# Two layers of attention and a 16-expert mixture on one core: four full sets of expert weights that go round, and each expert's blocks in one loop of their own in the second layer

## The reference

```python
SEQ = 256; CTX_LEN = 256; D_MODEL = 1024; DEPTH = 2
N_EXPERTS = 16; TOP_K = 2; EXPERT_FF = 512

def moe_ffn(h, router_w, router_bias, w_gate, w_up, w_down):
    ...
    _, exp_idx = lax.top_k(jnp.where(exp_mask, sel, NEG_INF), TOP_K)
    ...
    y = jnp.zeros_like(h)
    for e in range(N_EXPERTS):
        a = jax.nn.silu(h @ w_gate[e]) * (h @ w_up[e])
        y = y + gates[:, e:e + 1] * (a @ w_down[e])
    return y
```

## Time and profile before

| | us |
|---|---|
| median of 3 runs | 1149.88 (1148.8 to 1151.57) |
| the profiled execution, its own time | 1146.06 |
| its span, first to last instruction | 1144.2 |
| first mixture, TensorE's block work | about 418 to 649 |
| between (combination, second attention) | about 650 to 906 |
| second mixture | about 906 to 1136 |

### The profile page before, as it was taken

How to read it: one execution, slowest core, us unless ns; L and a number is a source line. 1 busy time by engine, 2 the same in 40 slices (tenths; PEclk the granted TensorE clock), 3 DMA queues, 4 the chain that set the end, 5 groups by cost and what they waited for, 6 DMA issues and landing times.

```text
span 1144.2 us, 25209 instructions
## 1 busy us (share of the span) xinstructions
PE 1004.0 (88%) x10134; PEld 660.9 (58%) x10135; DVE 411.6 (36%) x881; ACT 336.5 (29%) x755; POOL 173.1 (15%) x257
## 2 busy tenths in 40 slices
PE   4799999988889988799899649999999866999875
PEld 2577777544555565467566447888454643555543
DVE  1533331355843542122122273212862721323212
ACT  3532221366741211011111255323861110111111
POOL 0000000000000024244344300920000010112100
PEclk9999999999999999899899869999999897999988
DMA  9866664998240579999999467222627889699994
GB/s 338 303 219 221 221 210 171 346 355 314 109 199 18 208 280 399 422 421 424 422 424 415 172 248 164 94 74 104 264 60 306 335 320 425 253 381 425 424 423 188
DMA packets 90811, 317.58 MB, mean 278 GB/s; under 512 B 20094, under 2 KB 32135, under 8 KB 78451
## 3 DMA queue, kind: packets, MB, share of 16 engines
q1 hardware_dynamic: 84594, 303.04, 69.0%
q0 software_dynamic: 5280, 10.36, 2.4%
q10 hardware_dynamic: 864, 3.15, 0.7%
HBM read 311.05 MB, written 9.54 MB: 280 GB/s over the span
## 4 chain that ended last, share of the span: by engine, by line
PE 73%; DMA 14%; DVE 4%; issue 4%; ACT 3%; SPq 1%; DVEq 0%; ACTq 0%; POOLq 0%
PE ps L2031 25%; PE ps L1772 21%; PE ps L1927 7%; DMA expert_sets<-in_moe_w_up_dram 7%; PE ps L1669 5%; PE ps L1693 3%; DMA expert_sets<-in_moe_w_down_dram 2%; DMA ring<-in_ada_w_dram 2%; PE ps L2053 2%; PE ps L1827 1%; PE ps L1854 1%; DMA ada_late<-in_ada_w_dram 1%; PE ps L1883 1%; PE ps L1710 1%; DMA moe<-h_rows,slot_idx 1%
## 5 line engine op out<-in xcount | busy, mean ns | idle before, releaser
L2031 PE MATMUL ps<-expert_sets,moe 128*32 128x256 f32 x6304 | 363.7, 390 | 54.1 <-issue 31.2
L2031 PEld LDWEIGHTS ps<-expert_sets,moe 128*32 128x32 f32 x6304 | 226.5, 113 | 186.7 <-issue 76.5
L1772 PE MATMUL ps<-w_high,x_high 128*128 128x512 f32 x352 | 141.4, 402 | 6.6 <-DVE x_low L508 5.1
L1618 DVE STREAM_TRANSPOSE moe<-moe 128x256 f32<-128x256 f32 x68 | 44.7, 657 | 263.8 <-PE ps L2031 257.2
L1772 PE MATMUL ps<-w_high,x_low 128*128 128x512 f32 x352 | 137.9, 392 | 0.0
L1772 PE MATMUL ps<-w_low,x_high 128*128 128x512 f32 x352 | 137.7, 391 | 0.0
L1125 ACT ACTIVATE moe<-ps 128x128 f32<-128x128 f32 x68 | 18.9, 277 | 327.5 <-PE ps L2031 325.9
L495 DVE TENSOR_TENSOR w_low<-ring,w_high 128x2048 fp32r<-128x2048 f32 x24 | 56.2, 2350 | 132.5 <-ACT w_high L492 132.5
L1772 PEld LDWEIGHTS ps<-w_high,x_high 128*128 128x128 f32 x352 | 66.5, 189 | 30.5 <-issue 14.8
L779 POOL MEMSET moe<- 128x128 f32 x2 | 0.4, 204 | 534.9 <-PE ps L1953 534.9
L797 POOL DMA_INDIRECT moe<-h_rows,gather_idx x66 | 68.4, 1037 | 52.2 <-POOL gather_idx L843 27.7
(11 more groups left out here) (261 smaller groups left out, 1143.1 us busy)
## 6 DMA issues: line engine op xcount, KB each, us to landing
expert_sets<-in_moe_w_down_dram SPq DMA_DIRECT2D x32, 2048.0 KB, 18.4
expert_sets<-in_moe_w_gate_dram SPq DMA_DIRECT2D x30, 2048.0 KB, 15.9
expert_sets<-in_moe_w_up_dram SPq DMA_DIRECT2D x30, 2048.0 KB, 21.0
ring<-in_ada_w_dram SPq DMA_DIRECT2D x16, 2048.0 KB, 8.0
ring<-in_diff_w_qkv_dram SPq DMA_DIRECT2D x6, 2048.0 KB, 9.3
ada_late<-in_ada_w_dram SPq DMA_DIRECT2D x6, 2048.0 KB, 12.4
ring<-in_na_w_qkv_dram SPq DMA_DIRECT2D x6, 2048.0 KB, 8.9
rows<-mod_rows SPq DMA_DIRECT2D x11, 512.0 KB, 7.3
```

The lines of the kernel that those rows point to most:

```text
L1618: dve.transpose(blk_inT, blk_in[b].rearrange("p (j k) -> p k j", k=KC)).then_inc(m_xt[l], 1)
L1772: mm = pe.matmul(ps[:, n % 2], x_part[:, k, tok], w_part, start=(k == 0 and i == 0), stop=(k == KC - 1 and i == 2))
L2031: mm = pe.matmul(ps[g * SLOTS:(g + 1) * SLOTS, bank, 0:n_out], lhs_T[:, k, :], weights(k, g), start=(k == 0), stop=(k == n_chunks - 1), sk ...
```

## The change

There are now four full sets. The extra pair gets a down matrix beside it (`extra_down`, 16 KB a partition), for which room is made behind the residual rows: it also covers the rows of modulation values and the rotary tables, both of which have been used by then, and the scratch area for the descriptors of GpSimd's transfers shrinks to 1024 bytes a partition. Every position uses set (position modulo 4). Its loads wait for the position four before. The down matrix of position 3 is loaded ahead: in the first layer right after the modulation rows of the second layer have been stored, in the second layer behind the attention strips. The outer loops hold four positions and run three times in both layers.

In the second layer the order of TensorE changes: for every block, gates and ups of that block, the sums of the preceding block, the downs of that same block, in one loop per position. VectorE weighs the preceding block's result at the start of its step rather than at the end. The code of positions 13 to 15 and the special last position go. The strips of the second attention take slots 0, 1, 2 in turn, so that the first two wait for gates and ups of position 14 and the third for its downs.

The diff, cut to its core:

```diff
-EXTRA = 3
+SETS, EXTRA = 4, 3
...
+        extra_down = over("extra_down", ARENA_KB + 16, [P, FF // P, D])
...
-                    add_qkv(g, (i + 2) % 3)
+                    add_qkv(g, i % 3)
...
+        def loads(l, p, rounds=0):
+
+            return 16 * (p // SETS + 1 + rounds + l * (N_EXP // SETS))
...
-            def later_parts(l, p, which, ws, back=3):
+            def later_parts(l, p, which):
                 e = expert_at(l, p)
-                for w in ws:
+                blocks = sp.value_load(plan[0:1, bass.ds(p + 1 - SETS, 1)], min_val=1, max_val=MAX_BLOCKS)
+                for w in range(3):
                     if w != 1:
-                        blocks = sp.value_load(plan[0:1, bass.ds(p + 1 - (3 if w == 2 else back), 1)], min_val=1, max_val=MAX_BLOCKS)
                         sp.wait_ge((m_gu, m_gu, m_dn)[w][l], blocks + (w == 2))
                         sp.sem_inc(s_turn_sp, 1)
-                    expert_weights(l, w, e, which[w == 2])
+                    expert_weights(l, w, e, which)
...
-                later_parts(l, EXTRA + 1, (gate_set(EXTRA + 1), None), (0, 1), back=4)
-                later_parts(l, EXTRA, (None, EXTRA % 3), (2,))
-                later_parts(l, EXTRA + 1, (None, (EXTRA + 1) % 3), (2,))
-                for p in range(5, 7):
-                    later_parts(l, p, (gate_set(p), p % 3), (0, 1, 2), back=4)
-                with sp.Fori(0, (N_EXP - 7) // 3) as i:
-                    for p in range(7, 10):
-                        later_parts(l, 3 * i + p, (gate_set(p), p % 3), (0, 1, 2))
+                with sp.Fori(0, N_EXP // SETS - 1) as i:
+                    for s in range(SETS):
+                        later_parts(l, SETS * i + SETS + s, s)
...
+            sp.wait_ge(s_modD, 32)
+            expert_weights(0, 2, EXTRA, EXTRA)
...
+            expert_weights(1, 2, EXTRA, EXTRA)
             sp.wait_ge(s_qm[1], len(qkv_jobs[1]))
...
                     for b in range(2):
+                        if l == 1:
+                            dve.wait_ge(m_dn[1], 2 * j + b + 1)
+                            weigh_rows(2 * j + b)
                         dve.wait_ge(m_ga[l][1 - b], 16 * j + 16)
...
-                        if l == 1:
-                            weigh_rows(2 * j + b)
...
+                def blocks_summed(p, first, end, rounds=0):
+
+                    with pe.Fori(first, end) as i:
+                        gates_ups(i, p % SETS)
+                        sum_rows(i)
+                        down_loaded(p, rounds)
+                        downs(i, p % SETS)
...
+                def expert_summed(p, first, end, rounds=0, then=None):
+
+                    after = None if then is None else block_end(then)
+                    gates_loaded(p, rounds)
+                    pe.sem_inc(s_turn_pe, 1)
+                    blocks_summed(p, first, end, rounds)
                     return after
...
-                keep_busy((5, 14)[l])
+                keep_busy((5, 10)[l])
...
-    nc = bacc.Bacc("TRN2", target_bir_lowering=False, num_devices=1)
+    nc = bacc.Bacc("TRN2", target_bir_lowering=False, num_devices=1, dynamic_dma_scratch_size=1024)
```

More of the change, by code:

```diff
@@ L362, in build_trunk @@
         s_idx = [sem(f"plan_ready_{l}") for l in range(LAYERS)]
-        m_wl = [[sem(f"expert_{w}_loaded_{s}") for w in ("gate", "up", "down")] for s in range(3)]
-        s_extra = sem("extra_parts_loaded")
+        m_wl = [[sem(f"expert_{w}_loaded_{s}") for w in ("gate", "up", "down")] for s in range(SETS)]
         s_keep = sem("residual_rows_kept")
@@ L729, in _ @@
             sp.dma_start(mod_dram[1].ap(), mod_rows[:]).then_inc(s_modD, 16)
-            last_blocks, n0 = load_experts(0)
-            sp.wait_ge(m_dn[0], last_blocks + 1)
-            load_strip(1, 0)
-            load_expert_rows(0, n0)
-            blocks = sp.value_load(plan[0:1, N_EXP:N_EXP + 1], min_val=N_EXP, max_val=MAX_BLOCKS)
+            sp.wait_ge(s_modD, 32)
+            expert_weights(0, 2, EXTRA, EXTRA)
+            blocks, pairs = load_experts(0)
             sp.wait_ge(m_gu[0], blocks)
-            for j in range(1, 3):
+            for j in range(2):
                 load_strip(1, j)
+            sp.wait_ge(m_dn[0], blocks + 1)
+            load_strip(1, 2)
+            load_expert_rows(0, pairs)
             sp.wait_ge(s_cb[0], NT[0])
@@ L1709, in keep_busy @@
                 for _ in range(count):
-                    pe.matmul(ps[:, 3, 0:2 * P], ident, cst[:, 0:2 * P], start=True, stop=True)
+                    pe.matmul(ps[:, 3, 0:2 * P], ident, cst[:, P:3 * P], start=True, stop=True)
             for a in range(ADA_QKV):
@@ L2105, in expert @@
                     down_loaded(p - 1, rounds)
-                    downs(first - 1, (p - 1) % 3)
-                    sum_rows(first)
+                    downs(first - 1, (p - 1) % SETS)
                     with pe.If(first + 1 < end):
@@ L2128, in _ @@
                     weight_table()
-                keep_busy((5, 14)[l])
+                keep_busy((5, 10)[l])
                 pe.wait_ge(s_idx[l], 2)
                 ends = [block_end(0), block_end(1)]
+                if l == 1:
+                    sum_rows(0)
+                    down_loaded(0)
+                    downs(0, 0)
                 with pe.If(1 < ends[0]):
                     down_loaded(0)
-                    with pe.Fori(1, ends[0]) as i:
-                        gates_ups(i, 0)
-                        downs(i - 1, 0)
-                        sum_rows(i)
@@ L2138, in _ @@
-                for p in range(1, 4):
-                    ends.append(expert(p, ends[p - 1], ends[p], then=p + 1 if p < 3 else None))
-                with pe.Fori(0, (N_EXP - 4) // 3 - l) as three:
-                    end_0, end_1 = block_end(3 * three + 3), block_end(3 * three + 4)
-                    end_2 = expert(4, end_0, end_1, three, 3 * three + 5)
-                    end_3 = expert(5, end_1, end_2, three, 3 * three + 6)
-                    expert(6, end_2, end_3, three)
-                if l == 1:
-                    end_0, end_1 = block_end(N_EXP - 4), block_end(N_EXP - 3)
-                    end_2 = expert(N_EXP - 3, end_0, end_1, then=N_EXP - 2)
-                    end_3 = expert(N_EXP - 2, end_1, end_2, then=N_EXP - 1)
-                    last_expert(N_EXP - 1, end_2, end_3)
+                    pe.sem_inc(s_turn_pe, 1)
@@ new lines, in _ @@
+                    if l == 1:
+                        blocks_summed(0, 1, ends[0])
+                    else:
+                        with pe.Fori(1, ends[0]) as i:
+                            gates_ups(i, 0)
+                            downs(i - 1, 0)
+                turn_of = (expert, expert_summed)[l]
+                for p in range(1, SETS):
+                    ends.append(turn_of(p, ends[p - 1], ends[p], then=p + 1 if p + 1 < SETS else None))
+                with pe.Fori(0, N_EXP // SETS - 1) as i:
+                    end_0, end_1 = block_end(SETS * i + SETS - 1), block_end(SETS * i + SETS)
+                    end_2 = turn_of(SETS, end_0, end_1, i, SETS * i + SETS + 1)
+                    end_3 = turn_of(SETS + 1, end_1, end_2, i, SETS * i + SETS + 2)
+                    end_4 = turn_of(SETS + 2, end_2, end_3, i, SETS * i + SETS + 3)
+                    turn_of(SETS + 3, end_3, end_4, i)
```

77 lines of the change are left out of this document (23 added, 54 removed).

## The result

The changed kernel takes **1123.81 us**, median of 5 runs (1119.17 to 1125.81), against 1149.73 (1148.67 to 1151.57) for the kernel before in the same session: a ratio of 0.9773 (95% interval 0.9755 to 0.9792). The forecast was 1123.5. The profiled execution took 1119.17 us with a span of 1117.3, where before it was 1146.06 and 1144.2.

The account below looks back on a forecast made before the run. TensorE and DMA bound the first mixture, late-started loads the second's end. Terms -5.5 (first mixture), -19.5 (second), -1.3 (tail) sum to -26.3: 1119.8 profiled, plus 3.8 to the median gives 1123.5 us; 8-in-10 range 1114 to 1138.

Parts of the forecast that it names:

- First mixture: Layer-0 mixture: one load leaves the saturated stretch, so the last up lands 5.5 us earlier; -5.5 us, ends -7.5 and 0.
- The loads of the second mixture: Second mixture: SyncE's queue no longer stands still during position 5's six blocks; loads end at 1096 to 1106, before 1129.
- The open turn: Second mixture: each block's downs wait for VectorE's turned activation, 0.40 us a block uncovered by the sums, ends 0 and 1.5.
- Entries into the outer loop: Second mixture, TensorE: three entries at 2.3 us each, with a third register read, 1.80 each before; 6.9 us.
- First pass of code: Second layer, TensorE: stalls when code runs the first time; 5 us taken, ends 0 and 16.
- Lowered clock: Second mixture: one set of gates slowed behind a first-code stop, 7.17 us instead of 5.32; 1.8 us.
- Tail: Behind the last downs: one sum instead of two, 2.0 us for weighing and sum; -1.3 us.
- The longer loop body does not stay: Rival, 8%: layer 0's four-position loop no longer stays on the chip, two more first passes; +10.6 us, 1134.
- First pass as before: Rival, 10%: the second layer's first pass stalls as before, 16 us instead of 5; +11 us, 1134.5.
- the turn longer than its pieces: Rival, 10%: the second mixture's turn leaves 0.9 us open a block instead of 0.4; +13 us, 1136.5.
- The clock falls: Rival, 7%: TensorE's stops in every second-mixture block lower its clock; nine blocks low cost 58 us, 1181.
- Scratch area: Rival, 3%: the smaller area makes GpSimd wait, about 7 us more per layer-0 block if one transfer fits; far above 1300.

Follow-up runs that it names:

- the ends carried: Changed kernel, with TensorE carrying the outer loop's two starting block ends in registers from the preceding pass, both layers: 1120.1 us, ratio 0.9735 to the kernel before.
- the two experiments on the turn: Changed kernel, second layer: VectorE turns the same rows once more (1136.74 us), or turns the activation ahead of the next block's rows (1117.54 us).
- changed again: A later run of the changed kernel, with nothing altered: 1124.17 us, ratio 0.9781 to the kernel before.
- the order alone: Kernel before with its three sets, places and loads, but the second layer's blocks in the new order: 1144.35 us, ratio 0.9953.
- the sets alone: Changed kernel with four sets, but the second layer's blocks in the old order with a branch over each position's loop: 1169.3 us, ratio 1.0181.
- the shorter turn: Changed kernel; in the second layer VectorE multiplies and turns the activation before the next block's rows: 1117.54 us, in a second run 1119.2 us.

## Why the prediction was right

The sum was -26.3, the two profiled executions differ by 26.9.

- **First mixture, -5.5 foreseen, -7.6 measured** (239.4 to 231.8). The pair of profiles flatters it: the eight that share the changed first mixture's code have 231.8 to 236.8, 233.1 on the mean, and the three of the old code 238.8 to 239.4, so -5.9. Right in kind: the last up lands some 7 us earlier. The step that failed is its cause, that the load was issued early: issued late, it costs nothing that can be measured. The step on the register reads of the outer loop ("at nothing") held: with the ends carried this mixture took 232.2.
- **The loads of the second mixture.** Foreseen: no standstill of SyncE, last down at 1096 to 1106 less 5.5. It landed at 1098.6, in that range, but the standstill is there, longer than before. The step "SyncE stands still no more" was wrong as worded: the nine loads, issued from 930.00 to 948.90, were queued by the time the six blocks began, and they bridge it. (The upper bound is 1105 by the prediction's own terms, not 1106.)
- **The open turn, 0.40 a block foreseen, 0.37 measured**, and the two experiments on the turn move the time one for one. A block takes 6.84 us (967.53 to 974.37), 6.80 foreseen.
- **Entries into the outer loop, 6.9 foreseen, 5.9 measured** (1.77, 2.09, 2.04). At the steps between positions the downs and the next gates take 5.6 us instead of 5.4, about the 0.15 foreseen.
- **First pass of code, 5 foreseen, 1.4 measured.** Mis-sized: the only stop that is not a register read is 1.43 us, and 2.31 at the same place in "changed again". (That profile has another of 1.91 us ahead of the fillers, but it costs nothing: the first sums start 12.5 us behind the first gates in both.) **Lowered clock, 1.8 foreseen, 1.7 measured** (gates of 5.35 instead of 3.66 behind the second entry), but behind register reads and not behind first code.
- **What the sum lacked.** At the start of the second mixture the granted clock fell to 0.70 on the mean, part of the stretch at the lower of its two levels (1.2 GHz instead of 2.4). In the kernel before it was 1.00 from 911.6 to 921 us (below, first the changed kernel):

```profile
911.60:921.00 9.40, 7.90 (x87) 4.09 (x91) 1.80 (x5) 0.00 (x0) 1.21 (x2) 0.70 0.92 389
```

```profile
911.60:921.00 9.40, 6.89 (x56) 5.24 (x59) 5.86 (x22) 1.65 (x3) 3.25 (x4) 1.00 0.84 319
```

  TensorE had stood 3.58 us for VectorE's weighing ahead of the first sums, behind fewer filler products than before (20 MATMUL instead of 28, of `keep_busy((5, 10)[l])`). The first sums took 2.09 us instead of 1.15, and the next gates about 2 more: some 3 us. It ate most of the 3.6 us that the first pass of code did not cost. That the fewer fillers are the cause is not shown, and the order alone speaks against it: it keeps the 28 (`keep_busy((5, 14)[l])`), stood only 1.87 us ahead of these sums, and they took 1.75 us. "Changed again" has 20, stood 1.41 us, and its sums took 1.15:

```profile
919.25 1.15 PE L2046 MATMUL ps<-moe 32*128 32x256 f32 x16 [1.41 <-DVE moe L1604]
```

- **Tail, -1.3 foreseen, -1.05 measured.**

**The rivals.** *The longer loop body does not stay*: it stays here with 4 x 96 products in the first layer, with jumps of 0.22 us back and a branch of 0.08 over the loops in the later passes:

```profile
L2077 PEldq COMPARE_BRANCH  x7: 68/80/5802, 430.3 to 509.1; - x7
...
L2077 PEldq COMPARE_BRANCH  x8: 68/78/83, 526.1 to 626.1; - x8
```

It was given 8%, and the margin was small: at most 16 products a position. Its price of 10.6 us was far too low for a body that does not stay, if the second layer is a guide: there 56 unused products a position cost some 60 us, most of it in stops of up to 13 us, and the sets alone lost 20 us to the kernel before. *First pass as before*, *the turn longer than its pieces*: not seen. *The clock falls*: not by the open turns, even at 0.9 us each. *Scratch area*: nothing.

The sum of what was measured: -0.6 ahead of the first mixture, -7.6, +1.5 between the mixtures (256.6 to 258.1), -19.1, -1.05, together -26.9. So the total was right partly because errors cancel: the first pass of code against the clock at the start of the second mixture, and the first mixture's 2 us more against the 1.5 us between the mixtures, which the sum did not have. Some of these terms differ between profiles of the same kernel: in "changed again" the first code cost 2.3 us and the clock held at the start, with 205.7 us for the mixture; and between the mixtures the kernels with the old first mixture show 256.6 to 257.8, "changed again" 260.5. That the forecast of 1123.5 met 1123.81 to 0.3 us is luck; the changed kernel's runs spread over 7 us.

## What to carry to other kernels

A loop's code has a length at which every pass becomes a first pass. Count the products in the body ahead of widening a rotation, and let a block's code stand once in it: here the reorder paid mainly by halving the body, and the wider rotation without it lost 20 us. Of a chain with two bounds that lie close together (TensorE and the transfers), an edit of one side pays only until the other ends last: the shorter turn and the carried ends gave 4 to 5 us each in the second mixture, and together nothing more, so that three different kernels end at 0.973 to 0.974. Around a short turn between engines, put what the waiting engine needs ahead of what only the next block needs.

## What the runs showed of the hardware

- A body of 4 x 96 products of the program stays with TensorE, one of 4 x 112 doesn't. In the trace each is two MATMUL and two LDWEIGHTS, so 1,536 such instructions do and 1,792 don't. (Registers and branches are not counted in.) The jump back costs 0.21 us in the one case, 6.2 to 6.7 in the other, with the DMA engines busy 0.95 to 1.01 of the time around it. Code that is jumped over and never run counts: the 56 unused products show it. A packet of the instruction queue is 0.51 MB / 31 = 16 KB. The Trainium skill, "Runtime: NRT & Kernel Launch", section "Instruction fetch mechanics", states 128 KiB for TensorE, 2048 instructions, in blocks of 16 KiB: the size of a packet agrees, and the body that no longer stays, 1,792 without its registers and branches, lies below that figure. The same section says that a taken branch outside the current two-page window is a fetch; for TensorE the rows above differ, since later passes of a body of 1,536 jump back in 0.21 us.
- Read ahead of an empty queue, a register costs TensorE 0.7 us.
- Waiting for an engine in every block, 0.4 or 0.9 us of 7, left the granted clock at 1.00, the level of 2.4 GHz. Behind single stops of 2.09, 3.58 and 5.42 us it fell: gates of 5.35 and 6.47 us instead of 3.66, sums of 2.09 instead of 1.15. But the length of the stop alone does not decide. "Changed again" has two entries with a stop of 2.04 us; behind the one at 1025.58 the gates took 3.66 us, behind the one at 1076.03 5.35. With the order alone a stop of 2.01 us (1092.85) lowered it and one of 2.10 (1012.91) did not, and the kernel before stayed at 1.00 behind 2.40 us (918.95). What decides stays open.
